# Rounds 2 to 6 of five feed-forwards as seven block products of 256 tokens in place of eight

## The reference

```python
D_MODEL, SEQ, D_FF = 1024, 512, 2816

def swiglu(h, w1, w3, w2):
    return (jax.nn.silu(h @ w1) * (h @ w3)) @ w2

def half_ffn(x, g, w1, w3, w2):
    return x + FFN_RES * swiglu(rmsnorm(x, g), w1, w3, w2)

def swiglu_2(h, w_gate_up, w_down):
    g, u = jnp.split(h @ w_gate_up, 2, axis=-1)
    return (jax.nn.silu(g) * u) @ w_down
...
h = rmsnorm_2(x, norm2_w[l]) * (1.0 + sc2) + sh2
x = x + g2 * swiglu_2(h, w_gate_up[l], w_down[l])
```

## Time and profile before

| | us |
|---|---|
| three runs | 3152.40, 3152.54, 3154.52 |
| median | 3152.54 |
| the profiled execution, its own time | 3152.74 |
| its span, first to last instruction | 3150.9 |
| TensorE busy | 3141.7 |
| VectorE busy | 1871.2 |
| ScalarE busy | 1168.8 |

### The profile page before, as it was taken

How to read it: one execution, slowest core, us unless ns; L and a number is a source line. 1 busy time by engine, 2 the same in 40 slices (tenths; PEclk the granted TensorE clock), 3 DMA queues, 4 the chain that set the end, 5 groups by cost and what they waited for, 6 DMA issues and landing times.

```text
span 3150.9 us, 36008 instructions
## 1 busy us (share of the span) xinstructions
PE 3141.7 (100%) x14688; PEld 2594.4 (82%) x14688; DVE 1871.2 (59%) x2685; ACT 1168.8 (37%) x1644; POOL 157.8 (5%) x170
## 2 busy tenths in 40 slices
PE   9999999999999999999999999999999999999999
PEld 8888878888888888888888888887888888788887
DVE  5567467446855467557644685988533368863332
ACT  5322264322233222264422223665322235742221
POOL 2000000000000000000000000122000002300000
PEclk9999999999999999999999999999999999999999
DMA  5345422334542345432232463221232332022322
GB/s 151 98 130 194 125 84 90 96 103 145 188 131 80 99 131 180 139 94 81 92 96 94 147 200 110 84 68 41 96 102 93 100 89 81 28 94 94 106 87 74
DMA packets 334331, 339.79 MB, mean 108 GB/s; under 512 B 12502, under 2 KB 329208, under 8 KB 334168
## 3 DMA queue, kind: packets, MB, share of 16 engines
q1 hardware_dynamic: 332144, 333.80, 33.1%
q0 software_dynamic: 1792, 3.62, 0.4%
q10 hardware_dynamic: 232, 0.06, 0.0%
HBM read 335.36 MB, written 2.10 MB: 107 GB/s over the span
## 4 chain that ended last, share of the span: by engine, by line
PE 93%; DVE 4%; ACT 3%; issue 0%; POOL 0%; DVEq 0%; POOLq 0%
PE ps L138 91%; PE ps L141 2%; ACT ar L95 1%; DVE ar L108 1%; DVE wl L100 1%; DVE ar L100 1%; ACT wh L95 0%; DVE T L108 0%; DVE hl L108 0%; ACT L95 0%; ACT sp L95 0%; DVE ar L123 0%; DVE ar L111 0%; ACT T L95 0%; DVE ar L105 0%
## 5 line engine op out<-in xcount | busy, mean ns | idle before, releaser
L138 PE MATMUL ps<-hh,wl 128*128 128x512 f32 x2760 | 1081.1, 392 | 0.4 <-DVE wl L100 0.4
L138 PE MATMUL ps<-hh,wh 128*128 128x512 f32 x2760 | 1074.5, 389 | 0.0
L138 PE MATMUL ps<-hl,wh 128*128 128x512 f32 x2760 | 1074.1, 389 | 0.0
L100 DVE TENSOR_TENSOR wl<-raw,wh 128x1024 fp32r<-128x1024 f32 (+3 forms) x549 | 653.9, 1193 | 585.7 <-ACT wh L95 585.1
L95 ACT ACTIVATE wh<-raw 128x1024 fp32r<-128x1024 f32 (+3 forms) x549 | 560.4, 1024 | 452.7 <-PE ps L138 452.1
L138 PEld LDWEIGHTS ps<-hh,wl 128*128 128x128 f32 x2760 | 518.2, 188 | 112.4 <-issue 5.3
L138 PEld LDWEIGHTS ps<-hh,wh 128*128 128x128 f32 x2760 | 518.1, 188 | 108.2
L138 PEld LDWEIGHTS ps<-hl,wh 128*128 128x128 f32 x2760 | 518.4, 188 | 105.5 <-issue 0.2
L138 PE MATMUL ps<-ul,wh 128*128 128x512 f32 x1152 | 440.5, 389 | 0.0
L138 PE MATMUL ps<-uh,wl 128*128 128x512 f32 x1056 | 412.0, 390 | 0.0
L138 PE MATMUL ps<-uh,wh 128*128 128x512 f32 x1056 | 411.0, 389 | 0.0
(11 more groups left out here) (253 smaller groups left out, 2666.1 us busy)
## 6 DMA issues: line engine op xcount, KB each, us to landing
raw<-in_ffn_w SPq DMA_DIRECT2D x119, 1024.0 KB, 5.3
raw<-in_w_ada SPq DMA_DIRECT2D x48, 1024.0 KB, 5.2
raw<-in_w_gate_up SPq DMA_DIRECT2D x44, 1024.0 KB, 5.1
raw<-in_m_w_in SPq DMA_DIRECT2D x26, 1024.0 KB, 5.4
raw<-in_w_down SPq DMA_DIRECT2D x16, 1024.0 KB, 4.9
raw<-in_ffn_w SPq DMA_DIRECT2D x16, 768.0 KB, 4.2
raw<-in_w_in SPq DMA_DIRECT2D x12, 1024.0 KB, 5.4
raw<-in_m_w_out SPq DMA_DIRECT2D x8, 1024.0 KB, 4.9
```

Of the source, the lines that this page charges most:

```text
L100: return self.issue(lambda e: e.tensor_tensor(out, a, b, op))
L138: return self.issue(lambda e: e.matmul(out, l, r, start=start, stop=stop, skip_group_check=True))
```

## The change

In five of the six feed-forwards (all but the first), the ten weight chunks of rounds 2 to 6 (w1 and w3 of each) are no longer done as two runs. A chunk is taken as 2 x 2 blocks of 512 rows by 128 columns, and the activations as 2 x 2 blocks of 512 channels by 256 tokens. The product of two such matrices takes eight block products, and Strassen's scheme in Winograd's form takes seven, of sums of blocks. These are the "parts" 1 to 7. A part is 4 x 3 matmuls of 256 columns.

- The weights' sums are made by VectorE in place in `raw`: four subtractions or additions of 4 x 128 elements per chunk (`mixed_weights`), as soon as the block that is overwritten has been split. Each part's weights are split by themselves, 512 elements, into half a buffer of `wh` and `wl`; `room` and `before` give the half and the part that used it last. So six halves are in turn.
- The activations' four sums are made once per stage (`differences`): `full` is `hh + hl` (two instructions of 2048 elements), then four of 1024 (`diff`), four copies to `diff_h` by ScalarE, four subtractions to `diff_l`. They are issued beside the products of rounds 0 and 1.
- TensorE gathers parts 1, 6 and 7 in a bank X, adding up, and parts 4 and 5, then 3 and 2, in a bank Y. ScalarE copies X (256 columns) after part 1, 6 and 7, into `sq` and `acc`; TensorE waits for the first copy before part 6, for the second before part 7. The odd tile is Y (parts 4, 5) plus the third copy, the even tile Y (parts 2, 5 + 3) plus the first two. VectorE adds them (`joined`), and TensorE waits for the odd one (`odd`) before part 3.
- Parts 3 and 2 of a chunk come after parts 1, 4, 6, 5 of the next.
- In "ffn" the sum is then multiplied by R in an instruction of its own, and in both kinds a w3 tile by the gate in one more.

```diff
+FFNS = (("ffn", 0, 0), ("ffn", 0, 1), ("ffn", 1, 0), ("ffn", 1, 1), ("ffn2", 0), ("ffn2", 1))
+WOVEN = {s: {(w, j) for j in range(2, 7) for w in ("w1", "w3")} if s != ("ffn", 0, 0) else set() for s in FFNS}
+PARTS = (1, 4, 6, 5)
+SHARE = {1: (0, 0), 5: (0, 0), 3: (0, 0), 2: (1, 0), 4: (1, 1), 6: (1, 1), 7: (0, 1)}
+MOVING = {5: 0, 6: 1, 7: 2, 4: 3}
...
+def rounds(s):
+    left = None
+    for j in range(11):
+        for w in ("w1", "w3"):
+            if (w, j) in WOVEN[s]:
+                for p in PARTS:
+                    yield "part", w, j, p
+            else:
+                yield "run", w, 2 * j, 0
+            if left:
+                yield "part", *left, 3
+                yield "part", *left, 2
+                yield "joined", *left, 0
+                left = None
+            if (w, j) in WOVEN[s]:
+                yield "part", w, j, 7
+                yield "joined", w, j, 1
+                left = w, j
+            else:
+                yield "post", w, 2 * j, 0
+                yield "run", w, 2 * j + 1, 0
+                yield "post", w, 2 * j + 1, 0
...
+        room, before, halves, filled = {}, {}, [0], {}
+        for o in order:
+            if o[0] != "mm":
+                continue
+            g = o[1]
+            some = 1 if g in part_of else 2
+            halves[0] += halves[0] % 2 if some == 2 else 0
+            at = [(halves[0] + i) % (2 * SUBS) for i in range(some)]
+            before[g] = max(filled.get(i, -1) for i in at)
+            filled.update((i, g) for i in at)
+            room[g] = at[0] // 2, 512 * (at[0] % 2)
...
+        def quarter_of(n, p):
+            k, f = SHARE[p]
+            return raw_view(n)[:, 4 * k:4 * k + 4, 128 * f:128 * f + 128]
         def split_views(g):
             n, c, w, t0, tn = shape[g]
-            hi = wh[g % SUBS][:, 0:tn * w].rearrange("p (t n) -> p t n", t=tn)
-            lo = wl[g % SUBS][:, 0:tn * w].rearrange("p (t n) -> p t n", t=tn)
+            b, o = room[g]
+            if g in part_of:
+                hi = wh[b][:, o:o + 512].rearrange("p (t n) -> p t n", t=4)
+                lo = wl[b][:, o:o + 512].rearrange("p (t n) -> p t n", t=4)
+                return hi, lo, quarter_of(n, c)
+            hi = wh[b][:, 0:tn * w].rearrange("p (t n) -> p t n", t=tn)
+            lo = wl[b][:, 0:tn * w].rearrange("p (t n) -> p t n", t=tn)
             return hi, lo, raw_view(n)[:, t0:t0 + tn, c:c + w]
...
+                g = G_of[(s, w, j, "part", p)]
+                step(g)
+                if p == 1:
+                    banks.take((s, "X", w, j), True)
+                elif p == 4:
+                    banks.take((s, "Y", w, j), True)
+                b = ps((s, "X" if p in (1, 6, 7) else "Y", w, j))
+                c = slice(256, S) if p in (3, 5) else slice(0, 256)
+                hi, lo = weights(g)
+                if p == 6:
+                    pe.wait_ge(curved, (s, "p1", w, j))
+                elif p == 7:
+                    pe.wait_ge(curved, (s, "p16", w, j))
+                elif p == 3:
+                    pe.wait_ge(worked, (s, "odd", w, j))
+                for k in range(4):
+                    if p in MOVING:
+                        pe.wait_ge(hi_part, (s, "diff", MOVING[p]))
+                        pe.wait_ge(lo_part, (s, "diff", MOVING[p]))
+                        a_h, a_l = diff_h[:, MOVING[p], k, :], diff_l[:, MOVING[p], k, :]
+                    else:
+                        t, h = {1: (k, 0), 2: (4 + k, 0), 3: (4 + k, 256)}[p]
+                        operand((s, "h"), t)
+                        a_h, a_l = hh[:, t, h:h + 256], hl[:, t, h:h + 256]
+                    done = pe.three(b[:, c], hi[:, k, :], lo[:, k, :], a_h, a_l, k == 0 and p in (1, 4, 2), k == 3)
...
             def step(g):
-                while at[0] < len(mms) and at[0] <= g + 2:
+                while at[0] < len(mms) and before[at[0]] < g:
                     i = at[0]
                     at[0] += 1
                     hi, _, src = split_views(i)
                     act.wait_ge(raw_in[shape[i][0] % RAW], shape[i][0])
-                    if i >= SUBS:
-                        act.wait_ge(used, i - SUBS)
+                    if i in part_of and part_of[i][3] in (3, 5, 6, 7):
+                        act.wait_ge(worked, (*part_of[i], "weights"))
+                    if before[i] >= 0:
+                        act.wait_ge(used, before[i])
                     act.f(hi, src, ACT.Copy).then_inc(hi_split, i)
...
+            def differences(s):
+                yield 1
+                yield 1
+                for some in ((0, 2), (1, 3)):
+                    for c in some:
+                        act.wait_ge(worked, (s, "diff", c))
+                        act.f(diff_h[:, c, :, :], diff[:, c, :, :], ACT.Copy).then_inc(hi_part, (s, "diff", c))
+                    yield 1
+            def woven_part(s, w, j, p):
+                g = G_of[(s, w, j, "part", p)]
+                step(g)
+                act.advance()
+                pq = sq[woven_at[s, w, j] % 2]
+                b = ps((s, "X", w, j))
+                if p == 1:
+                    act.wait_ge(used, g)
+                    act.f(pq[:, 0:256], b[:, 0:256], ACT.Copy).then_inc(curved, (s, "p1", w, j))
+                elif p == 6:
+                    act.wait_ge(used, g)
+                    act.f(pq[:, 256:S], b[:, 0:256], ACT.Copy).then_inc(curved, (s, "p16", w, j))
+                elif p == 7:
+                    act.wait_ge(used, g)
+                    act.f(acc[:, 0:256], b[:, 0:256], ACT.Copy).then_inc(left((s, "X", w, j)), (s, "X", w, j))
...
+            def mixed_weights(s, w, j, p, n):
+                def mix(dst, a, b, op):
+                    dve.tt(quarter_of(n, dst), quarter_of(n, a), quarter_of(n, b), op).then_inc(worked, (s, w, j, dst, "weights"))
+                if p == 1:
+                    mix(7, 1, 7, SUB)
+                elif p == 4:
+                    dve.wait_ge(worked, (s, w, j, 7, "weights"))
+                    dve.wait_ge(lo_split, G_of[(s, w, j, "part", 4)])
+                    mix(6, 4, 7, SUB)
+                    dve.own()
+                    mix(5, 6, 1, ADD)
+                elif p == 7:
+                    dve.wait_ge(lo_split, G_of[(s, w, j, "part", 5)])
+                    mix(3, 2, 6, SUB)
...
-                    if (o[1] > g + 2) if o[0] == "mm" else (g < 2):
+                    if (before[o[1]] >= g) if o[0] == "mm" else (g < 2):
                         return
                     at[0] += 1
                     if o[0] == "mm":
                         hi, lo, src = split_views(o[1])
                         dve.wait_ge(hi_split, o[1])
                         dve.tt(lo, src, hi.bitcast(F32), SUB).then_inc(lo_split, o[1])
+                        if o[1] in part_of:
+                            mixed_weights(*part_of[o[1]], o[2])
...
+            def joined(s, w, j, a):
+                t = 2 * j + a
+                to = (T1 if w == "w1" else T3)[a][:, :]
+                y = ps((s, "Y", w, j))
+                dve.wait_ge(*((worked, (s, "gv", t - 2)) if w == "w1" else (lo_part, (s, "u", t - 2))))
+                if a:
+                    v = acc[:, 0:256].unsqueeze(1).to_broadcast([128, 2, 256])
+                    dve.wait_ge(*left_of((s, "X", w, j)))
+                    dve.tt(to.rearrange("p (l n) -> p l n", l=2), y[:, :].rearrange("p (l n) -> p l n", l=2), v, ADD).then_inc(worked, (s, "odd", w, j))
+                else:
+                    dve.wait_ge(used, G_of[(s, w, j, "part", 2)])
+                    dve.wait_ge(curved, (s, "p16", w, j))
+                    dve.tt(to, y[:, :], sq[woven_at[s, w, j] % 2][:, :], ADD).then_inc(left((s, "Y", w, j)), (s, "Y", w, j))
+                if s[0] == "ffn":
+                    dve.own()
+                    dve.tt(to, to, R[:, :], MUL).then_inc(worked, (s, "gate" if w == "w1" else "value", t))
+                if w == "w3":
+                    dve.own()
+                    silu_done(s, t)
+                    dve.tt(to, to, T1[a][:, :], MUL).then_inc(worked, (s, "gv", t))
...
+            def differences(s):
+                for h in range(2):
+                    r = slice(4 * h, 4 * h + 4)
+                    for t in range(4 * h, 4 * h + 4):
+                        dve.wait_ge(hi_part, (s, "h", t))
+                        dve.wait_ge(lo_part, (s, "h", t))
+                    dve.tt(full[:, r, :], hh[:, r, :].bitcast(F32), hl[:, r, :].bitcast(F32), ADD).then_inc(worked, (s, "full", h))
+                yield 1
+                b11, b12, b21, b22 = (full[:, 4 * h:4 * h + 4, c:c + 256] for h in range(2) for c in (0, 256))
+                dve.own()
+                dve.tt(diff[:, 0, :, :], b12, b11, SUB).then_inc(worked, (s, "diff", 0))
+                dve.tt(diff[:, 2, :, :], b22, b12, SUB).then_inc(worked, (s, "diff", 2))
+                yield 1
+                dve.wait_ge(worked, (s, "diff", 0))
```

(9 more changed lines are left out.)

## The result

The changed kernel takes 3196.82 us (median; 3152.58 for the kernel before on the same chip), a ratio of 1.0137 with a 95% interval of 1.0123 to 1.0151. Four executions stand behind that median: 3195.01, 3196.18 and 3197.46 us, and a slow one of 3858.71 at a mean granted clock of 0.75, which the ratio leaves out. The forecast was 3184 with a range of 3156 to 3216. The profiled execution took 3195.01 us, its span is 3193.2.

The account below looks back on a forecast made before the run. VectorE was to set the pace in ffn rounds after a late start, where TensorE bounds the kernel now. Three ffn lose 39 us, two ffn2 gain 8: 31 more than 3152.74 gives 3184 us, range 3156 to 3216.

Parts of the forecast that it names:

- TensorE's price: Changed weight blocks on TensorE: 256-column matmuls follow in 0.120 us, 10.1 us a block against 10.9, saving 39 us.
- by the page alone: TensorE's saving by the skill page's formula, 109 ns for 256 columns: 86 us; the sum used the rows' 39 instead.
- VectorE's round: VectorE in changed rounds: 34 instructions, 23.2 us in ffn; 30 instructions, 20.3 us in ffn2; against 20.2 on TensorE.
- three waits: VectorE's round trips to ScalarE each round: gated tiles 0.2 twice, parts 6 and 5 0.4, w1's part 7 0.7 us.
- The start of ffn: Round 2 of each changed ffn: the differences' low halves are done at 1023.9, so TensorE waits about 8 us.
- The closing term: End of an ffn's changed rounds: last low half 0.7, part 7 itself 1.4, parts 3 and 2 2.9 us.
- third rival: Part 6 waits for a copy behind a gate, and clock may drop: 1 us more per round, 4 each start; 3221, chance 0.12.
- The start of ffn2: Round 2 of ffn2: VectorE about 2 us behind TensorE; each ffn2 still gains 4 us, twice 8.
- The clock: TensorE after the idle 8 us at each start: a lower clock would double 0.120 for some parts; within a 0.12 rival.
- the sum of 13: Each changed ffn: its rounds end at 1135.9 instead of 1122.9, a loss of 13 us, 39 for three.

Follow-up runs that it names:

- e_no_sums: The changed kernel without the sums and differences of weight quarters on VectorE, so parts 7, 6, 5 and 3 multiply plain quarters: 3148.02 us.
- e_copy_first: The changed kernel with ScalarE copying part 1 out before the pending even tile's gate or high half, whose low half on VectorE comes later too: 3181.29 us.
- e_ffn2_late: The changed kernel with only the two ffn2 stages changed, rounds 3 to 6, differences three products later and the two `full` sums in two products: 3143.35 us.
- e_from_3: The changed kernel with rounds 3 to 6 in seven parts and round 2 as before the change: 3170.86 us.
- v_pool: The changed kernel with rounds 3 to 6, part 1 copied first, differences later, and the sums for parts 7 and 3 on GpSimd: 3163.40 us.

## Why the prediction was right, and where it was not

**TensorE's price** held: 256 columns follow in 0.120 wherever nothing waits and the clock is full (1029.51 to 1029.63), and TensorE's rounds of 168 matmuls take 20.16 us in ffn2(0) (from 2315.50 to 2325.58 for one weight, 10.08) and 20.15 in e_no_sums. The 86 us given in the prediction as the saving "by the page alone" are a slip: they pair 0.109 for 256 columns with the trace's 0.227 for 512, and with the 0.216 given beside it they are 60. Nothing else rests on them.

**VectorE's round** held: 23.2 said and 23.3 seen in ffn, 20.3 and 20.4 in ffn2, 0.60 for a weight sum with 0.688 of duration. By parts: busy 65.83 / 3 = 21.9, idle 1.36, where the sum had 21.7 and 1.5. The two splits are not cut at the same place (the sum's 21.7 holds short pauses ahead of dependent instructions, which the trace counts as idle). e_no_sums, with e_copy_first, where VectorE fills 97% of the round, shows that its work is the cause, not merely equal to it. One of the three waits is to be seen as it was said, the low half of part 7 behind w1's odd Silu, which waits 0.62 (0.7 said). It is w3's part 7, where the prediction says w1's: TensorE comes to it 3.5 us later, at 1100.52, as the last part of w3 of round 4.

```profile
1097.02 0.69 DVE L100 TENSOR_TENSOR wl<-raw,wh 128x512 fp32r<-128x512 f32 x1 [0.62 <-ACT wh L95]
```

**The start of ffn** held: last low half of the differences said for 1023.9 on the time of before, 1038.28 with the shift of 14.38 that the trace has by then. TensorE's gap ends at 1038.22. It waits 8.3 us, 8 said.

**The closing term was too small.** From the low half of part 7 of the last weight I allowed 5.0 us. It is issued at 1143.62, and part 7 ends at 1148.56. Parts 3 and 2 come behind a run of round 7, at 1154.03; their 2.9 us put behind part 7, as the sum had them, the same point is 1151.4, so 7.8. TensorE isn't waiting for that part 7 when its low half is issued: it starts part 6 of the same weight only at 1141.29, held back by the copy of part 1. That wait was in the third rival (part 6 behind a gate that waits for VectorE), and it comes seven times in each ffn. But it doesn't add 1 us to the round of 23.2, as the rival had it. It only puts TensorE behind VectorE, which shows once, at the end. The low half itself came 1.7 us earlier than said (1145.3 with the shift): the first half round took 9.7 us (1040.70 to 1050.43), where the same half takes 12.0 a round later (1061.73 to 1073.72), since no even tile of a weight before it was pending. So two errors partly cancel, and 1.1 of the 2.8 remain. They are most of the 1.4 by which each ffn exceeded 13.

**The start of ffn2 was the wrong step.** -4 each was said, -0.5 and -0.3 came. VectorE's walk was right to within half a microsecond (low half of part 7 at 2303.27, 2303.7 with the shift). I took TensorE as following VectorE with one closing term, though there TensorE needs 20.16 us a round and trails it. From 2308.24 to the end of the rounds TensorE is busy without a gap, so all that it lost before that point stays lost: 2.1 us at 2281.05, 1.6 of half clock behind it, 2.1 ahead of part 6 and 1.2 ahead of part 7 of the first changed weight. That is 7.1 of the 8.0 that ten weights save; where the last 0.4 lies isn't shown. In ffn2(1) the losses are as large but lie otherwise: 2.2 us of wait with no half clock behind it, then 3.3 ahead of a part 6 with half clock behind that. I had written that the start puts VectorE 2 us behind TensorE, and treated it as absorbed. e_ffn2_late gets 4.8 a stage by beginning a round later and making the sums later; e_from_3, which only begins a round later, gets 1.0 and 2.0.

**The clock** stood in the third rival alone, and in no term. It came at all five starts. In ffn 4.5 to 5.6 of its 10.2 us lie in time that TensorE waits anyway. In ffn2 it costs 1.6 us each. At half clock 256 columns follow in 0.21, not in double 0.120.

Together: 3 x 1.4 + 3.5 + 3.7 = 11.4 us. The profiled execution is 11.0 above 3184, and the median another 1.8 above that, which no trace explains. The direction, and the order of the two causes (rate of VectorE, lateness at the start), were as said; e_from_3 divides the 14.4 of an ffn into 6.6 for four rounds and 7.8 for a fifth that starts too early. In the ffn the sum of 13 is near 14.4 partly by luck, as two errors of 1.7 and 2.8 us have opposite signs.

## What to carry to other kernels

Before an exchange of TensorE's work for VectorE's, count VectorE's instructions in the stretch and multiply them by their step (0.60 us for 512 elements here), not by the share of the whole span. Then ask where the one-time work goes: 4.4 us of VectorE in one piece, in a stage where each weight tile has little lead, stopped TensorE for 2 us, and in some traces half clock for 3.4 us came right behind. The same change, put only where VectorE has room, one round later and with that work spread, gained 0.3% instead of losing 1.4%, and 0.4% with two of the four sums of a weight on GpSimd.

## What the runs showed of the hardware

Half clock was there at each of the long gaps of TensorE in these traces (3.4 to 9.8 us from matmul to matmul, 26 of them). Behind shorter ones it came in part of the cases: the gap of 2.35 us ahead of a low half stands in ten ffn2 stages of five traces, and half clock begins within 1.3 us behind it in five of them. It also came in a stage that no kernel changed, in four of the fourteen traces, where TensorE counts as busy. In e_from_3 it is busy for all of 160.0 to 171.1 and then at half clock:

```profile
160.00:171.10 11.10, 11.10 (x58) 9.24 (x57) 5.03 (x9) 1.66 (x3) 0.00 (x0) 1.00 0.23 71
171.20:174.50 3.30, 3.30 (x9) 2.56 (x8) 2.42 (x8) 0.65 (x2) 0.00 (x0) 0.50 0.24 85
```

What TensorE does just before is little work, though:

```profile
168.54 1.94 PE L138 MATMUL ps<-VT,ar 8*128 8x1 f32 x16
```

Sixteen matmuls of one column fill those 1.9 us. The kernel before has the same row (at 167.71) and no half clock behind it. It costs 1.6 us of the 2.4 that this execution has lost by its first w2 (259.2 instead of 256.8); e_copy_first, e_no_sums and v_pool have the same. What decides whether half clock comes is open, here as behind the gaps of 2.35 us.

GpSimd's 512-element sum of two SBUF tiles takes 1.3 us and more (two in 3.0), and costs VectorE beside it 0.7 us each in the rows shown, more than the 0.60 that VectorE needs to do it itself. In these kernels it paid only in ffn2, where VectorE has time to spare.
